# A conditioning matvec in four column groups of the array, its rows turned by full transposes and summed on VectorE

## What is computed

```python
def _layer(x, cvec, rows, s0, l, p):
    mod = jnp.einsum('bd,de->be', jax.nn.silu(cvec), p['ada_w'][l]) + p['ada_b'][l]
    sh1, sc1, g1, sh2, sc2, g2 = [m[:, None, :] for m in jnp.split(mod, 6, axis=-1)]
    h = _rmsnorm(x, p['norm1_w'][l]) * (1 + sc1) + sh1
    mix, s_fin = _mixer(h, rows, s0, l, p)
    x = x + g1 * mix
    h = _rmsnorm(x, p['norm2_w'][l]) * (1 + sc2) + sh2
    x = x + g2 * _convffn(h, rows, l, p)
```

## Time and profile before

| what | value |
|---|---|
| runs, median (lowest, highest) | 1004.87 us (1003.56, 1005.1) |
| span of the profiled execution | 1001.4 us |
| TensorE busy | 979.4 us, 98% |
| VectorE busy | 644.8 us, 64% |
| ScalarE busy | 346.6 us, 35% |
| matvec matmuls (line 1178), sum of their rows | 72.4 us in 160 rows |

### The profile page before, as it was taken

One profiled execution on the slowest core, in us unless ns is written; L12 is line 12 of the kernel. 1 busy time (PEld: TensorE's weight loads), 2 busy tenths in 40 slices (PEclk: granted clock), 3 DMA queues, 4 the chain that ended last, 5 costly groups with the idle time before them and its releaser, 6 DMA issues.

```text
span 1001.4 us, 13700 instructions
## 1 busy us (share of the span) xinstructions
PE 979.4 (98%) x5628; PEld 835.9 (83%) x5628; DVE 644.8 (64%) x815; ACT 346.6 (35%) x590; POOL 0.2 (0%) x4
## 2 busy tenths in 40 slices
PE   7999999999999999999999999999999999999996
PEld 1257899999999994288849999988999988899985
DVE  4883458787786976947367656644566654466665
ACT  2552543444435313042164343311333331133333
POOL 0000000000000000000000000000000000000000
PEclk9999999999999999999999999999999999999999
DMA  7815332111211112824251212222122221121102
GB/s 288 329 72 173 122 126 85 49 43 44 80 52 44 48 48 98 294 81 154 99 210 43 85 47 80 85 84 85 43 85 84 84 85 68 59 85 63 45 20 105
DMA packets 17559, 97.01 MB, mean 97 GB/s; under 512 B 1912, under 2 KB 4472, under 8 KB 7257
## 3 DMA queue, kind: packets, MB, share of 16 engines
q1 hardware_dynamic: 17496, 96.14, 26.8%
HBM read 92.98 MB, written 3.15 MB: 96 GB/s over the span
## 4 chain that ended last, share of the span: by engine, by line
PE 93%; DVE 3%; ACT 2%; issue 1%; DMA 0%; SPq 0%; ACTq 0%; DVEq 0%
PE ps L1159 24%; PE ps L1161 24%; PE ps L1160 24%; PE ps L1178 7%; PE ps L1365 3%; PE ps L1484 1%; PE ps L1267 1%; PE ps L1377 1%; PE ps L1205 1%; PE ps L1297 1%; PE ps L1457 1%; PE ps L1258 1%; PE ps L1472 0%; PE ps L1385 0%; PE ps L1354 0%
## 5 line engine op out<-in xcount | busy, mean ns | idle before, releaser
L1159 PE MATMUL ps<-h_hi,w_hi 128*128 128x320 f32 x1152 | 360.8, 313 | 0.6 <-DVE h_lo L779 0.6
L1161 PE MATMUL ps<-h_hi,w_lo 128*128 128x320 f32 x1152 | 356.5, 309 | 0.0
L1160 PE MATMUL ps<-h_lo,w_hi 128*128 128x320 f32 x1152 | 356.3, 309 | 0.0
L771 DVE TENSOR_TENSOR w_lo<-raw,w_hi 128x1024 fp32r<-128x1024 f32 x114 | 138.8, 1225 | 140.8 <-ACT w_hi L487 135.9
L1159 PEld LDWEIGHTS ps<-h_hi,w_hi 128*128 128x128 f32 x1152 | 216.5, 188 | 1.6 <-DVE h_lo L779 0.9
L1160 PEld LDWEIGHTS ps<-h_lo,w_hi 128*128 128x128 f32 x1152 | 216.5, 188 | 0.3
L1161 PEld LDWEIGHTS ps<-h_hi,w_lo 128*128 128x128 f32 x1152 | 216.3, 188 | 0.0
L487 ACT ACTIVATE w_hi<-raw 128x1024 fp32r<-128x1024 f32 x114 | 118.7, 1051 | 134.4 <-PE ps L1161 128.1
L1159 PE MATMUL ps<-w_hi,a_hi 128*128 128x512 f32 x220 | 86.9, 395 | 0.0
L1160 PE MATMUL ps<-w_lo,a_hi 128*128 128x512 f32 x220 | 86.9, 395 | 0.0
L1161 PE MATMUL ps<-w_hi,a_lo 128*128 128x512 f32 x220 | 86.9, 395 | 0.0
(11 more groups left out here) (252 smaller groups left out, 1081.2 us busy)
## 6 DMA issues: line engine op xcount, KB each, us to landing
raw<-in_slots SPq DMA_DIRECT2D x76, 1024.0 KB, 4.8
xin<-in_x_sample SPq DMA_DIRECT2D x4, 512.0 KB, 6.9
x<-in_x_sample SPq DMA_DIRECT2D x4, 512.0 KB, 5.6
out_y_sample<-x SPq DMA_DIRECT2D x4, 512.0 KB, 2.6
decay<-in_decay SPq DMA_DIRECT2D x1, 1280.0 KB, 12.1
ktab<-in_ktab SPq DMA_DIRECT2D x1, 1024.0 KB, 6.8
utab<-in_utab SPq DMA_DIRECT2D x1, 1024.0 KB, 4.8
itab<-in_itab SPq DMA_DIRECT2D x1, 1024.0 KB, 4.9
```

Source lines behind the costliest of these rows:

```text
L771: V.tensor_tensor(w_lo[:, n % SPLITS, :], raw[:, s % RAWS, u * UNIT:(u + 1) * UNIT], w_hi[:, n % SPLITS, :].bitcast(F32), ALU.subtract).th ...
L1159: mm(out, lhs[0], rhs[0], start=first, stop=False)
L1160: mm(out, lhs[0], rhs[1], start=False, stop=False)
L1161: return mm(out, lhs[1], rhs[0], start=False, stop=last)
```

## The change

The stationary operand is widened to 128x32: `silu_c` gets 32 columns, of which columns 0 and 1 hold the vectors and the rest are zero (one more memset at the start). The four calls of a part now write four different groups of 32 partitions of the bank, each from its own 32 columns of the array, and each group sums only two slices (one of either part). ScalarE copies all 128 partitions out. `ada_turn` makes four full 128x128 transposes into a whole bank (`TURN_BANK`), and VectorE sums the four groups with one reduction per block (`sum_groups`) into `mod`; the bias is added to that. As the banks are used again, a turn waits for the sum of the earlier block in its bank (`ada_taken`): turns 1, 2 and 3 for the sums of blocks 0, 1 and 2. The sums of blocks 0 and 1 stand in VectorE's list behind `sides(3)` and `sides(4)`, that of block 2 behind the scaling of x, that of block 3 at the old bias sum; the other sums stand in `ada_columns`. The inverse transform c = 1 waits for the first eight sums. The scaled identity `eyes` and its load go; the diagonal step of a head takes `ident` and a scale instead.

```diff
@@ -21,6 +21,7 @@
 U8 = mybir.dt.uint8
 ALU = mybir.AluOpType
 ACT = mybir.ActivationFunctionType
+AX = mybir.AxisListType
 
 P = 128
 D = 1024
@@ -46,6 +47,8 @@
 EPS = 1e-6
 SCALE = P ** -0.5
 UNIT = 1024
+GROUP = 32
+GROUPS = P // GROUP
 RAW = 2
 RAWS = 3
 SPLITS = 3
@@ -155,7 +158,6 @@
 
     c = {}
     c["ident"] = np.eye(P, dtype=np.float32)
-    c["diag"] = (np.eye(P) * SCALE).astype(np.float32)
     i, j = np.arange(P)[:, None], np.arange(P)[None, :]
     c["masks"] = np.stack([((i >> (l + 1)) == (j >> (l + 1))) & ((i >> l) != (j >> l))
                            for l in range(LEVELS)], 1).astype(np.uint32)
@@ -230,7 +232,7 @@
         ident = sb(ctx, "ident", [P])
         ones = sb(ctx, "ones", [P])
         eps = sb(ctx, "eps", [1])
-        silu_c = sb(ctx, "silu_c", [KD, 2])
+        silu_c = sb(ctx, "silu_c", [KD, GROUP])
         silu_parts = sb(ctx, "silu_parts", [KD, 4], F32R)
         mod = sb(ctx, "mod", [6 * KD, 2])
         gain = sb(ctx, "gain", [2, KD, 2])
@@ -268,7 +270,6 @@
         x2 = sb(mid, "x2", [NC, CONV])
         u_hy = sb(mid, "u_hy", [NC, T])
         hg = ExitStack()
-        eyes = sb(hg, "eyes", [P])
         masks = sb(hg, "masks", [LEVELS, P], U8)
         qs = sb(hg, "qs", [T])
         KK = sb(hg, "KK", [2, T])
@@ -363,6 +364,7 @@
 
         ADA_ROWS = [row_e] * 4 + [row_h] * 4 + [row_l] * 2
         ROW_BANK = (2, 2, 0, 1, 6, 5, 6, 5, 6, 5)
+        TURN_BANK = (3, 3, 3, 3, 7, 4, 3, 2, 7, 6)
         V_BANKS = (2, 3, 0, 1, 4)
 
         def fine_rows(f):
@@ -437,7 +439,6 @@
             eng.wait_ge(sem("h_split"), KD)
             eng.wait_ge(sem("kspec_ready"), 5)
             load(ap(QQ, 0, [(P, LEVELS), (1, P)]).bitcast(U32), io["masks"], "ld_hg")
-            load(eyes[:, :], io["diag"], "ld_hg")
             load(state0[:, :, :, :], io["state_hgrn"][0, 0].rearrange("d h k w -> k d h w"), "ld_hg")
             for s in range(ADA1 + RAWS, SLOT_ADA2 + 2):
                 slot(s)
@@ -502,7 +503,7 @@
                 eng.wait_ge(sem("ada_used"), 2 * b + 2)
                 if b >= 2:
                     eng.wait_ge(sem("ada_cols"), b - 1)
-                A(ADA_ROWS[b][0:2, b % 2, :], ps[0:2, ROW_BANK[b], :], ACT.Copy).then_inc(sem("ada_row"), 1)
+                A(ADA_ROWS[b][:, b % 2, :], ps[:, ROW_BANK[b], :], ACT.Copy).then_inc(sem("ada_row"), 1)
 
             def row_norm(which, i, x, junk):
 
@@ -522,7 +523,7 @@
                   scale=gain[:, which, k, 1:2], bias=mod[:, sh, 1:2]).then_inc(sem("h_full"), 1)
 
 
-            eng.wait_ge(sem("ones_ready"), 2)
+            eng.wait_ge(sem("ones_ready"), 3)
             eng.wait_ge(sem("ld_vec"), 16)
             A(silu_c[:, :, 0], v("c", 0, KD), ACT.Silu)
             A(silu_c[:, :, 1], v("c_ctx", 0, KD), ACT.Silu).then_inc(sem("silu_c"), 1)
@@ -787,6 +788,7 @@
                                             op0=ALU.mult, op1=ALU.add), name)
 
             V.memset(ones[:, :], 1.0).then_inc(sem("ones_ready"), 1)
+            V.memset(silu_c[:, :, :], 0.0).then_inc(sem("ones_ready"), 1)
             V.memset(eps[:, :], EPS).then_inc(sem("ones_ready"), 1)
             eng.wait_ge(sem("ld_vec"), 16)
             lb = v("lb_f", 0, 2 * NC)
@@ -801,8 +803,8 @@
 
 
             eng.wait_ge(sem("silu_c"), 1)
-            link(V.tensor_copy(silu_parts[:, :, 0:2], silu_c[:, :, :]))
-            link(V.tensor_tensor(silu_parts[:, :, 2:4], silu_c[:, :, :], silu_parts[:, :, 0:2].bitcast(F32), ALU.subtract))
+            link(V.tensor_copy(silu_parts[:, :, 0:2], silu_c[:, :, 0:2]))
+            link(V.tensor_tensor(silu_parts[:, :, 2:4], silu_c[:, :, 0:2], silu_parts[:, :, 0:2].bitcast(F32), ALU.subtract))
 
 
             two_pi = 2.0 * math.pi
@@ -822,6 +824,13 @@
                     link(V.scalar_tensor_tensor(out=a, in0=q, scalar=-cc, in1=a, op0=ALU.mult, op1=ALU.add))
                 link(V.tensor_scalar(a, a, -3.1415925, 3.1415925, ALU.max, ALU.min), "arg_ready")
 
+            def sum_groups(n):
+
+                b = ADA_BLOCKS[n]
+                eng.wait_ge(sem("ada_cols"), n + 1)
+                link(V.tensor_reduce(mod[:, 4 * b:4 * b + 4, :],
+                                     ap(ps, TURN_BANK[n] * 512, [(P, 4), (1, 2), (GROUP, GROUPS)]), AX.X, ALU.add), "ada_taken")
+
             eng.wait_ge(sem("ld_decay"), 16)
             def damp(i):
                 eng.wait_ge(sem("taps_made"), i + 1)
@@ -849,17 +858,21 @@
                     damp(i + 1)
                 sides(i)
 
+                if i >= 3:
+                    sum_groups(i - 3)
+
             for i in range(NT):
                 eng.wait_ge(sem("norm_ready"), i + 1)
                 link(V.reciprocal(stat[:, 0, 1, i:i + 1], stat[:, 0, 1, i:i + 1]))
                 link(V.tensor_scalar(xin[:, i, :], xin[:, i, :], stat[:, 0, 1, i:i + 1], None, ALU.mult), "x_scaled")
 
+            sum_groups(2)
             eng.wait_ge(sem("tapsums"), 1)
             link(V.tensor_scalar(knorm[:, 0, :], ps[:, 4, 0:2 * NC], EPS, None, ALU.add))
             link(V.reciprocal(knorm[:, 1, :], knorm[:, 0, :]), "knorm_ready")
 
-            eng.wait_ge(sem("ada_cols"), 4)
-            link(V.tensor_tensor(mod[:, 0:2 * KD, :], ap(ps, 3 * 512, [(2, 2 * KD), (1, 2)]),
+            sum_groups(3)
+            link(V.tensor_tensor(mod[:, 0:2 * KD, :], mod[:, 0:2 * KD, :],
                                  ap(vec, VEC["ada_b"], [(1, 2 * KD), (0, 2)]), ALU.add))
             link(V.scalar_tensor_tensor(out=gain[:, 0, :, :], in0=mod[:, KD:2 * KD, :], scalar=1.0,
                                         in1=ap(vec, VEC["norm1"], [(1, KD), (0, 2)]), op0=ALU.add, op1=ALU.mult), "gain_ready")
@@ -918,7 +931,8 @@
 
                 if j == DIAG:
                     eng.wait_ge(sem("head_steps"), h * STEPS + j + 1)
-                    link(V.tensor_tensor(scores[:, :], banks(score_bank(j)), ap(eyes, 0, [(0, NT), (1, P)]), ALU.mult), "scores_taken")
+                    link(V.scalar_tensor_tensor(out=scores[:, :], in0=banks(score_bank(j)), scalar=SCALE,
+                                                in1=ap(ident, 0, [(0, NT), (1, P)]), op0=ALU.mult, op1=ALU.mult), "scores_taken")
                     return
                 l = j - LEVEL0
                 s = 1 << l
@@ -965,7 +979,7 @@
                     finish_head(h)
 
             eng.wait_ge(sem("v_bank"), NT)
-            eng.wait_ge(sem("ld_hg"), 48)
+            eng.wait_ge(sem("ld_hg"), 32)
             link(V.tensor_copy(masks[:, :, :], ap(QQ, 0, [(P, LEVELS), (1, P)]).bitcast(U32)))
             for i in range(2):
                 link(V.memset(padm[:, i, :], 0.0), "pad_zero" if i else None)
@@ -1005,10 +1019,11 @@
                 pass_k(*step_at(n))
                 step(*step_at(n))
 
-            def ada_columns(b0, b1, bank):
-
-                eng.wait_ge(sem("ada_cols"), ADA_BLOCKS.index(b1 - 1) + 1)
-                link(V.tensor_tensor(mod[:, 4 * b0:4 * b1, :], ap(ps, bank * 512 + 8 * b0, [(2, 4 * (b1 - b0)), (1, 2)]),
+            def ada_columns(b0, b1):
+
+                for n in range(ADA_BLOCKS.index(b0), ADA_BLOCKS.index(b0) + b1 - b0):
+                    sum_groups(n)
+                link(V.tensor_tensor(mod[:, 4 * b0:4 * b1, :], mod[:, 4 * b0:4 * b1, :],
                                      ap(vec, VEC["ada_b"] + 4 * b0, [(1, 4 * (b1 - b0)), (0, 2)]), ALU.add), "mod_ready")
 
 
@@ -1049,7 +1064,7 @@
             eng.wait_ge(sem("half_made"), NH)
             link(V.tensor_copy(h_hi[:, 0:NC, :], o_hg[:, :, :]))
             link(V.tensor_tensor(h_lo[:, 0:NC, :], o_hg[:, :, :], h_hi[:, 0:NC, :].bitcast(F32), ALU.subtract), "heads_split")
-            ada_columns(4, 8, 7)
+            ada_columns(4, 8)
             for c in range(NC):
                 eng.wait_ge(sem("z_ready"), c + 1)
                 link(V.scalar_tensor_tensor(out=grid(zc, 0), in0=rows64(u_hy[:, c, 0:TS]), scalar=v("hy_d", c),
@@ -1104,7 +1119,7 @@
             norm_rows(NT - 1)
             split_lo(UNIT_FFN)
             split_lo(UNIT_FFN + 1)
-            ada_columns(10, 12, 7)
+            ada_columns(10, 12)
             for k in range(KD):
                 split_h(1, k)
             for i in range(2):
@@ -1173,19 +1188,19 @@
                 for i in parts:
                     slot = ADA_SLOTS[2 * b + i]
                     arrived(eng, slot)
-                    for kk in range(4):
-                        k = 4 * i + kk
-                        last = mm(ps[0:2, bank, :], silu_c[:, k, :], raw[:, slot % RAWS, kk * HW:(kk + 1) * HW],
-                                  start=(k == 0), stop=(k == KD - 1))
+                    for g in range(GROUPS):
+                        last = mm(ps[g * GROUP:(g + 1) * GROUP, bank, :], silu_c[:, GROUPS * i + g, :],
+                                  raw[:, slot % RAWS, g * HW:(g + 1) * HW], start=(i == 0), stop=(i == 1))
                     last.then_inc(sem("ada_used"), 1)
 
-            def ada_turn(b, bank):
+            def ada_turn(b):
 
                 eng.wait_ge(sem("ada_row"), b + 1)
```

(25 more changed lines are left out.)

## The result

The changed kernel takes 1007.55 us (median of nine runs, 1005.38 to 1009.09) against 1004.97 for the kernel before (nine runs, 1003.17 to 1005.1): ratio 1.0027, 95% interval 1.0018 to 1.0035. It is slower by 2.6 us; the forecast was 3.2 us faster, with a range that ended at 1006.5.

What follows compares the result with a forecast made beforehand. TensorE, with 93% of the chain, was taken as the bound. Terms +0.4-1.65-1.9 = -3.15 us on a 1001.4 us span, with 3.5 us between span and run, gave 1001.7 us; range 998.3 to 1006.5.

Steps and rivals of the forecast that it cites:

- The part's cost: One of a matvec block's two slots of four calls: five steps, 2.14 us, between bounds of 0.86 and 3.43.
- Stage 1: Matvec spread through the first 54 us: +0.4 us, with turn 1 waiting for VectorE's sum and low clock behind it.
- a low clock from 14.26: Bound for the first 54 us: clock already low when the second hidden layer is computed, making that stretch +1.7 us.
- Stage 2: Matvec at 395.7 to 425.2 us: VectorE's copy, then its sums, release the inverse transforms; the second starts 1.65 us earlier.
- Stage 3: Matvec at 504.1 to 519 us: the first FFN slot's transfer sets the end, -1.9 us.
- the prediction's two bounds: For the matvec at 504.1 to 519 us: all parts overlapping -2.95 us; low clock at the following transposes 1.4 worse.
- At nothing: ScalarE's row copies, the projection's diagonal step, one load less and one memset: put at no cost.
- The clock stays low longer: Rival: low clock around 42 to 54 us and after 421 and 515; 1004.4 to 1007.4 us, chance 0.14.
- full overlap: Rival: all four column groups run together, 0.86 to 1 us a part; 999.4 to 1001.0 us, chance 0.28.
- the case without overlap: Rival: a part stays 3.43 us and the new waits for VectorE bite; 1011.3 us, chance 0.16.

## Why the prediction was wrong

*The part's cost: wrong.* Five steps (2.14 us) was the middle of my bounds; it is the lower end, two steps: 24 rows for three parts in 2.78 us, 0.93 a part, 3.7 times faster. The second row of a call does not keep the next call back: the four first rows start together, then the four second ones. The Trainium skill, "TensorE: Matmul & The Clock Gate", Part 3 (packing small matmuls), has matmuls in different column groups run concurrently; the trace agrees, and my reading of its order (starts strictly in sequence, hence five steps) was the error. It made the forecast too low in what each part frees, and so in how long TensorE stands idle: in the run with the sums one step earlier, where the first part starts at 7.06 as it did before, 5.19 us ahead of the second hidden layer, for the 2.9 of the prediction.

*Stage 1: the failing step.* It read "the clock was still high" for the second hidden layer and for the taps, and let the low clock begin at turn 1. Forecast +0.4, measured +6.95. The row it read this from is one of before, where 1.43 us of idleness lay ahead of the layer and the clock had come up at 11.44, during a first part of 5.74 us. The change took that work away (1.93 us) and left 2.99 us of idleness ahead of the layer, and the clock came up only at 55.71. The slow start of the first part before was no fall after idleness either: the first layer of the network, at 2.99, is as slow (1.96 us for two rows). By its own marks: turn 1 was to start at 42.2 and started at 50.61. Of these 8.4 us, 2.9 are damp(0), at 26.47 for 23.6 (the second layer came a good microsecond later, and taps(0) took twice as long), and 5.4 are VectorE's later waits for taps, 1.51, 2.47 and 1.44, which the sum had set to nothing. From turn 1 on, 10.0 us were needed where 11.9 were forecast, as the parts are shorter still. I had named a low clock from 14.26 as a bound, but priced it at the layer's own rows (+1.7) and not at the taps behind it, which VectorE's whole chain waits for. The same page of the Trainium skill, Part 1 (the clock gate), has the clock fall back in idle stretches; the runs agree in that turn 1 takes 1.09 us for 0.63 behind 5.25 us of idleness (parts issued four times) and behind 8.50 (first three fills only). By what the prediction says of that page the direction at least was to be had.

*Stage 2: mechanism right, size off.* The first inverse was to be released by VectorE's copy, 25.7 us behind the stage's start, and was (429.07 less 403.39). The sums were to end 31.8 us behind it, and did (435.16). The second inverse was to follow the sums; it followed 0.65 us later, since the first (6.40 us) ran at the low clock for 5.5 us, until 434.59, and not for 4.3 us: -1.08 for -1.65.

*Stage 3: mechanism right.* The first FFN slot is what sets it: its split starts 8.4 us behind the stage's start, before 11.8, so -3.4 for a forecast of -2.3; of that 1.7 us went at the low clock in the first two groups of gate products and the transposes between them (3.63 us from 523.21 on, for 1.95). Net -1.61 for -1.9, close to the prediction's two bounds taken together (-2.95 and +1.4).

*At nothing: right.* A sum takes 0.19 us a block in VectorE's list, 0.22 with its hand-over, as taken from its nearest row. The row copies on ScalarE take 0.58 to 0.60 us for 0.57 to 0.59, and the diagonal step 0.82 us as before, with nobody waiting for it. TensorE does wait for row copies, but not for their length: 0.72 us at 19.17 (0.68 before), and 2.03 at 521.66, where the copy stands behind the split of the first FFN slot in ScalarE's list.

*The rivals.* "The clock stays low longer" came true, at 0.14, and its 1007.4 is the measured time within 0.2; but that is luck: it was worked out from turn 1 on, while the larger loss lies ahead of it, and it was paired with slow parts, not with full overlap. The true case was two rivals at once: the faster the parts, the longer the idleness, and the longer the low clock. *The range* was said to leave out the case without overlap alone; ending at 1006.5, it also cut off the upper end of this rival. *The base* was also off: 3.5 us were set between span and run, where the profiled span belongs to a run of 1003.2, some 1.8 above it, so that stage times of a run below the median were taken for those of the median.

## What to carry to other kernels

Work taken off the engine that bounds a kernel leaves idle time on it; where this is TensorE, ask whether the work that is taken away is what brought the clock up, price everything behind each new idle stretch at the lower clock level, and follow it to the engines that wait for it (here 7 us against some 3 gained elsewhere). Before such a change is given up, put matmuls that nobody reads into the waits: here they turned +2.6 us into -6.3, and with fills in the later stages and the sums moved as well into -10.1. Each must fit the wait that it stands in: with one too short and others too long, 997.69 us stood for 994.70.

## What the runs showed that I had not expected

Calls with a 128x32 stationary in four column groups run wholly side by side also where each float32 call leaves two rows: four calls, eight rows, in 0.93 us for 3.43. The view of the granted clock reads 1.00 over the first 56 us of after although taps took 0.88 us a step for 0.43, because the trace's list of levels has no entry ahead of the first rise (55.71 us in after, 11.44 in before): at a program's start the distance of the steps, or that first entry, has to be read. And gaps of 0.5 to 0.7 us among transposes were followed by transforms at the low level (2.08 us for 1.12); fills in their place kept it.
